# Attention in a decoder step: half a period of lead for the scores, two heads' sums in turn, log weights in the softplus tile

## The reference, cut to what matters

```
z     = einsum('bqhd,bkhd->bhqk', qb, kb) * scale + bias
log_1m = where(mask, log_sigmoid(-z), 0.0)                      # mask: k_pos < q_pos
log_w = log_sigmoid(z) + cumsum(log_1m, reverse=True) - log_1m
w     = where(mask, exp(log_w), 0.0)
out   = einsum('bhqk,bkhd->bqhd', w, vb)
```

## Time and profile before

| | us |
|---|---|
| median of 3 executions | 2448.33 (2446.66 to 2449.82) |
| the profiled execution | 2448.8 |
| its span | 2447.1 |
| PE busy | 2401.9 |
| DVE busy | 1224.1 |
| ACT busy | 999.7 |
| the attention stretch of the loop, in the span | about 573 to 662 |

### The profile page before, as it was taken

How to read it: one execution, slowest core, us unless ns; L and a number is a source line. 1 busy time by engine, 2 the same in 40 slices (tenths; PEclk the granted TensorE clock), 3 DMA queues, 4 the chain that set the end, 5 groups by cost and what they waited for, 6 DMA issues and landing times.

```text
span 2447.1 us, 44037 instructions
## 1 busy us (share of the span) xinstructions
PE 2401.9 (98%) x18930; PEld 2185.9 (89%) x18930; DVE 1224.1 (50%) x1693; ACT 999.7 (41%) x1408; POOL 114.6 (5%) x232
## 2 busy tenths in 40 slices
PE   6999999999999999999999999999999999999998
PEld 4999999965699999999999999887777999999998
DVE  4533335755576332357533346745555657633345
ACT  4522234635466322346422245533223546522243
POOL 0000000121100000000000000011222100000000
PEclk8999999999999999999999999999999999999999
DMA  7555455775546654565755345554455456643254
GB/s 279 180 164 172 127 183 178 254 214 130 191 119 208 199 164 130 179 210 174 240 158 171 117 156 179 193 161 158 159 176 165 134 167 187 186 142 94 86 178 154
DMA packets 122660, 417.12 MB, mean 170 GB/s; under 512 B 23386, under 2 KB 27610, under 8 KB 122210
## 3 DMA queue, kind: packets, MB, share of 16 engines
q1 hardware_dynamic: 89538, 302.08, 39.1%
q10 hardware_dynamic: 17568, 61.87, 7.4%
q0 software_dynamic: 15360, 50.34, 6.3%
HBM read 390.84 MB, written 23.41 MB: 169 GB/s over the span
## 4 chain that ended last, share of the span: by engine, by line
PE 90%; DVE 4%; DMA 2%; ACT 2%; issue 1%; SPq 0%; POOLq 0%; POOL 0%; ACTq 0%; DVEq 0%
PE PS L1986 73%; PE PS L1381 3%; PE PS L1920 3%; PE PS L1950 2%; PE PS L1311 1%; DVE WL L2259 1%; DMA AFIRST<-in_w_ada 1%; PE PS L747 1%; PE PS L1265 1%; PE PS L1296 1%; PE PS L1306 1%; PE PS L1277 1%; PE PS L750 1%; PE PS L1360 1%; ACT WH L2089 1%
## 5 line engine op out<-in xcount | busy, mean ns | idle before, releaser
L2259 DVE TENSOR_TENSOR WL<-RAW,WH 128x1024 fp32r<-128x1024 f32 (+1 forms) x478 | 633.2, 1325 | 702.0 <-ACT WH L2089 701.5
L1986 PE MATMUL PS<-HH,WH 128*128 128x260 f32 x3432 | 800.6, 286 | 3.5 <-DVE QRS L1613 2.2
L1986 PE MATMUL PS<-HH,WL 128*128 128x260 f32 x3432 | 786.7, 283 | 0.0
L1986 PE MATMUL PS<-HL,WH 128*128 128x260 f32 x3368 | 770.4, 283 | 0.0
L2089 ACT ACTIVATE WH<-RAW 128x1024 fp32r<-128x1024 f32 (+1 forms) x478 | 542.5, 1136 | 413.8 <-PE PS L1986 274.2
L1986 PEld LDWEIGHTS PS<-HH,WH 128*128 128x128 f32 x3432 | 569.5, 188 | 38.1 <-issue 30.4
L1986 PEld LDWEIGHTS PS<-HH,WL 128*128 128x128 f32 x3432 | 569.7, 189 | 0.0
L1986 PEld LDWEIGHTS PS<-HL,WH 128*128 128x128 f32 x3368 | 557.9, 188 | 0.6 <-issue 0.2
L1986 PE MATMUL PS<-GH,WH 128*128 128x260 f32 x1408 | 387.3, 285 | 0.0
L1986 PE MATMUL PS<-GL,WH 128*128 128x260 f32 x1408 | 384.6, 283 | 0.0
L1986 PE MATMUL PS<-GH,WL 128*128 128x260 f32 x1408 | 383.9, 283 | 0.0
(11 more groups left out here) (334 smaller groups left out, 2321.8 us busy)
## 6 DMA issues: line engine op xcount, KB each, us to landing
RAW<-in_w_in SPq DMA_DIRECT2D x236, 512.0 KB, 3.6
RAW<-in_w_out SPq DMA_DIRECT2D x120, 704.0 KB, 4.1
AW<-in_w_ada ACTq DMA_DIRECT2D x114, 512.0 KB, 4.5
RAW<-in_w_odd SPq DMA_DIRECT2D x60, 512.0 KB, 3.6
RAW<-in_w_odout SPq DMA_DIRECT2D x30, 512.0 KB, 3.9
RAW<-in_w_even SPq DMA_DIRECT2D x28, 512.0 KB, 4.3
KV<-in_v_pages POOLq DMA_DIRECT2D x32, 256.0 KB, 4.7
SR<-in_ret_past POOLq DMA_DIRECT2D x32, 256.0 KB, 3.8
```

The source lines that it names most:

```text
L1986: last = nc.tensor.matmul(ps[:, x, 0:HT], w[:, k * P:(k + 1) * P], src[k0 + k][:, x, :], start=(begin and t == 0), stop=(end and t == 2))
L2259: nc.vector.tensor_tensor(low_, RAW[:, from_:from_ + w], high_.bitcast(F32), ALU.subtract).then_inc(lo_done, 1)
```

## The change

It does three things in the even layer's attention, and moves no work to another engine.

1. `log_weights` writes its result into `SP`, over the softplus values of the same block, instead of back into `ZS`; `weights` then works in place. So `ZS[h % 4]` is free for the scores of the pair two later as soon as the log weights of the same block have been taken.
2. `scores` run half a period further ahead: blocks 0 and 1 of pair t+2 are computed in the second half of period t, and blocks 2 and 3 of pair t+1 in the first half. `scores(1, 0)` and `scores(1, 1)` come before the loop.
3. The sums of a pair's two heads alternate block by block, each head with its own bank of `PS[1]`. Before, head 2t had its four blocks in the first half, and head 2t+1 in the second. `sum_rank(h, i)` gives the place of a sum in that order. The number of sums, scores, copies, table loads and DMAs stays the same.

Beside it, the output DMA of `UP` (whose place `ZD` takes) gets a semaphore of its own, `pool_out`, and is issued ahead of the `KP` output, and the copy into `ZD` waits for it alone.

```diff
         def biased_to(t, j):
-            return 8 if (t, j) == (1, 0) else 10 * t - 4 if j == 0 else 10 * t - 2 + 2 * j
+            return 4 * t + 4 if t < 1 else 10 * t + 2 * j
+        def sum_rank(h, i):
+            return 8 * (h // 2) + 2 * i + h % 2
+        def bank_free_at(t, j):
+            return biased_to(t, j - 1) if j else 8 if t == 1 else biased_to(t - 1, 3)
...
             def scores(t, j):
-                if t == PAIRS:
+                if t >= PAIRS:
                     return
-                pe.wait_ge(z_dve, biased_to(t, j))
+                pe.wait_ge(z_dve, bank_free_at(t, j))
...
-                n = 4 * h + i
+                n = sum_rank(h, i)
                 pe.wait_ge(lw_done, n - 1) if n >= 2 else pe.wait_ge(vp_evac, 4)
-                last = nc.tensor.matmul(PS[1][:, i % 2, 0:LEN[i]], TRI[:], SP[h % 4][:, OFF[i]:OFF[i] + LEN[i]],
+                last = nc.tensor.matmul(PS[1][:, h % 2, 0:LEN[i]], TRI[:], SP[h % 4][:, OFF[i]:OFF[i] + LEN[i]],
...
             scores_of_one()
+            scores(1, 0)
             ada_step("start", 0)
+            scores(1, 1)
             for t in range(PAIRS):
-                scores(t + 1, 0)
+                scores(t + 1, 2)
                 sums(2 * t, 0)
-                scores(t + 1, 1)
+                scores(t + 1, 3)
+                sums(2 * t + 1, 0)
                 if t:
                     values(t - 1)
                 sums(2 * t, 1)
-                scores(t + 1, 2)
-                sums(2 * t, 2)
+                sums(2 * t + 1, 1)
                 if t == 2:
                     gather(0)
-                scores(t + 1, 3)
-                sums(2 * t, 3)
+                scores(t + 2, 0)
                 if t < 3:
                     values_past(t)
                 ada_step("head", 2 * t)
-                for i in range(4):
-                    sums(2 * t + 1, i)
+                sums(2 * t, 2)
+                sums(2 * t + 1, 2)
+                scores(t + 2, 1)
+                sums(2 * t, 3)
+                sums(2 * t + 1, 3)
                 if t == 3:
                     values_past(3)
                 ada_step("head", 2 * t + 1)
...
             def weights(h):
-                act.wait_ge(lw_done, 4 * h + 4)
-                nc.scalar.activation(SP[h % 4], ZS[h % 4], ACT.Exp).then_inc(w_done, 1)
+                act.wait_ge(lw_done, sum_rank(h, 3) + 1)
+                nc.scalar.activation(SP[h % 4], SP[h % 4], ACT.Exp).then_inc(w_done, 1)
...
-                dve.wait_ge(s_done, 4 * h + i + 1)
-                z = ZS[h % 4][:, OFF[i]:OFF[i] + LEN[i]]
-                nc.vector.tensor_tensor(z, z, PS[1][:, i % 2, 0:LEN[i]], ALU.subtract).then_inc(lw_done, 1)
+                dve.wait_ge(s_done, sum_rank(h, i) + 1)
+                at_ = slice(OFF[i], OFF[i] + LEN[i])
+                nc.vector.tensor_tensor(SP[h % 4][:, at_], ZS[h % 4][:, at_], PS[1][:, h % 2, 0:LEN[i]],
+                                        ALU.subtract).then_inc(lw_done, 1)
...
-                if j == 0:
-                    after(dve, w_done, 2 * t - 2)
-                    if t == 1:
-                        dve.wait_ge(out_done, 96)
+                if (t, j) == (1, 0):
+                    dve.wait_ge(pool_out, 16)
                 for e in range(2):
+                    after(dve, lw_done, sum_rank(2 * t - 4 + e, j) + 1 if t > 1 else 0)
                     dve.wait_ge(z_done, 8 * t + 2 * j + e + 1)
...
             scored_one()
+            scored(1, 0)
+            scored(1, 1)
             nc.vector.tensor_copy(VSR[0:NS, :], PS[3][0:NS, 1, :]).then_inc(vs_ok, 1)
...
-                scored(t + 1, 0)
+                scored(t + 1, 2)
                 log_weights(2 * t, 0)
-                scored(t + 1, 1)
+                scored(t + 1, 3)
+                if t == 0:
+                    softplus(1)
+                log_weights(2 * t + 1, 0)
+                sized(t + 1, 0)
+                sized(t + 1, 1)
+                for e in range(2):
+                    log_weights(2 * t + e, 1)
                 if t:
                     low(t - 1)
...
+                scored(t + 2, 0)
                 ada_evac("head", 2 * t)
-                for i in range(2):
-                    log_weights(2 * t + 1, i)
+                for e in range(2):
+                    log_weights(2 * t + e, 2)
+                scored(t + 2, 1)
+                for e in range(2):
+                    log_weights(2 * t + e, 3)
                 if t < 3:
                     softplus(2 * t + 2)
```

31 lines of the change are left out of this document (11 added, 20 removed).

## The result

| us | before | after |
|---|---|---|
| median of 7 executions | 2448.33 (2446.66 to 2449.82) | 2458.43 (2455.44 to 2463.81) |
| profiled execution, span | 2448.8, 2447.1 | 2457.74, 2456.1 |
| first sum over cached keys (`ZN`) to first output projection | 90.8 | 100.7 |
| the rest of the span | 2356.3 | 2355.4 |

The ratio of the times is 1.0042, with a 95% interval from 1.0032 to 1.0052. The kernel is slower, by more than 0.2% even at the lower end of that interval. The forecast was 2453.9 us, the range ended at 2457.3. The direction was right, and the loss of 10.1 us is nearly twice the 5.6 forecast. The third line of the table says that, in the profiled executions, all of it lies in the stretch that the change touches (I call it the loop).

The account below looks back on a forecast made before the run. PE's list was taken to bound the attention stretch: new waits 10.0 us, less 3.8 of old waits and 0.6 of switches, net +5.6 on the profiled 2448.8, 0.5 lower for the median: 2453.9 us, range 2449.3 to 2457.3.

Parts of the forecast that it names:

- What bounds it, and the log weights in place: Attention stretch: PE's list bounds it, only its waits can be won; writing log weights into `SP` costs nothing.
- The start, +4.65: Start of the loop: PE waits 0.55, 0.5 and 1.2 us around pair 1's score blocks, 2.4 for head 1's softplus.
- The slices, +2.7: Conditioning steps: `w_ada` slices land late, by 1.0 us in the first period, 0.8 then 0.9 in the third.
- Softplus at the turn, +1.35: Turn into the third period: PE waits 1.35 us for a softplus behind both heads' last sums.
- DVE in the third period, +0.9: Third period: PE's next score block waits 0.9 us behind DVE's second softplus, OSM copy and score copies.
- Alternation: Sums of both heads: banks free 0.1 us late four times, +0.4; fewer switches between scores and sums, -0.6.
- What was to go, -3.8: Old PE waits between 572 and 662 us that disappear: 1.5, 1.0, 0.3, and 1.0 of weight loads.
- The step that failed: the clock, +3.4: Loop: the forecast sum counted no loss from half clock, leaving that to a rival.
- Rival B: Start of the loop: the clock falls in the new 2.4 us wait, losing up to 3.4 us, 2457.3; chance 0.09.
- A (the lead holds): From the second period on, later waits (5.35 us) vanish and only the start costs: 2448.6 us; chance 0.18.
- C: Conditioning steps: slices collide with POOL's page loads, two steps wait 1.7 us longer each, 2457.3; chance 0.07.
- D: Start of the loop: early banks are free in time too, so the kernel gets faster, 2446.3 us; chance 0.04.

Follow-up runs that it names:

- the start regrouped: Changed kernel with head 1's softplus ahead of the first log weight, and the v row's copy and bank clearing ahead of pair 1's score copies; 2456.34 us.
- all three regroupings: Changed kernel with head 1's softplus and v row copy early, third-period gather and its copy early, each period's first conditioning step before its second sums; 2451.7 us.
- the steps early: Changed kernel with each period's first conditioning step moved ahead of its second pair of sums; 2455.5 us.
- the alternation alone: Kernel before with log weights in place and a pair's two heads' sums taking turns, score blocks left in their old period; 2457.58 us, ratio 1.0032.
- the lead alone: Kernel before with log weights in place and scores half a period ahead, sums still head by head; 2450.79 us, ratio 1.0007.
- the order without the waits: Changed kernel's instructions with PE and DVE lists reordered so every step's producer is done early; 2441.99 us, ratio 0.9969 to the kernel before.
- the two kernels with added products: Unread products put in PE's waits: ten in the changed kernel, 2455.24 us; six in the one with early softplus, gather and conditioning steps, 2451.76 us.

## Why the prediction was wrong, point by point

- **What bounds it, and the log weights in place.** Right. Everything happened in PE's waits in the loop, and the in-place edit alone measured no difference.
- **The start, +4.65.** Nearly right. Forecast 0.55, 0.5, 1.2 and 2.4; measured 0.52, none, 1.23 and 2.28, together 4.03. The second was covered: the score block and the conditioning step in front ran at half clock and gave DVE its time. With the clock up there it was 0.57 (the start regrouped). The sign that was to prove this step wrong, a first sum of head 0 before 581 us, did appear (580.68), but the whole loop starts 2.8 us earlier in this execution; counted from its first product that sum starts after 12.3 us, and the forecast was 11.1.
- **The slices, +2.7.** Forecast 1.0, then 0.8 and 0.9; measured 0.29 and 0.61, then 0.69 and 0.60, 2.2 together. In the first period the lateness fell on both slices of the step, not on the second alone. Mechanism right, size 0.5 too high.
- **Softplus at the turn, +1.35.** Measured 1.09, with 0.44 in front of it for a bank.
- **DVE in the third period, +0.9.** Measured 0.78.
- **Alternation.** Two waits of 0.2 for log weights instead of 0.4 in four. PE's busy time rose by 3.0 where the clock took 3.4 by estimate, which leaves 0.4 for the switches; forecast 0.6. No run shows this term by itself: all three regroupings together, at full clock and with a few more switches, are busy 86.14 us, 0.2 more than the kernel before.
- **What was to go, -3.8.** This was 0.7 too much. It counted 1.0 us in which weight loads waited for log weights like waits of PE, but PE's own products went on meanwhile. The waits of its products that went are 0.99, 1.48 and 0.34, 2.8 together, and with all smaller gaps at most 3.1 of the loop's idle time.
- **Missed: the copy of the gathered rows, +1.1.** The prediction weighed the OSM copy and the jam of DVE at the start of this period, but not what stands behind them. It listed what each moved DVE instruction lets go for scores and sums, and left out `copy_turned`, which lets go the cached values. Counting every wait of PE against the new DVE list would have shown it: |z| twice, two log weights and `low` are 4.5 us of work (631.71 to 636.17) in front of it. Moving the copy back took the wait away.
- **The step that failed: the clock, +3.4.** The sum took TensorE at full clock throughout, and put the half clock at nothing. The runs showed two stretches of 3.4 us at half clock, by which PE's busy time rose by 3.0, and added products that kept it at 1.00. Rival B had that loss (3.4 us) and came nearest with 2457.3, but by luck: it gave itself a chance of 0.09 and meant one long stretch at the one long wait, and its sign, a clock below 1.00 between 585 and 600 us, did not appear. At 584 to 588 us the clock stayed at 1.00 in the changed kernel; it fell at 574.1, after waits of 1.1 and 0.2 us and within one of 0.5, and at 645.8 behind 0.2, 0.7 and 0.6, with PE's products in between. The reading of the earlier trace rows, that a wait of 2.2 leaves the clock alone, is right of that wait in that execution. It doesn't carry over to several short ones. In other kernels of this study the clock fell behind the long wait after all (at 584.8 with the steps early, at 581.5 in the alternation alone), and in neither of these had it fallen earlier in the loop.
- **The sum.** Waits were forecast at +6.2 and came out at +6.9. That they are so close is partly luck: the new ones came to 10.0 as forecast, but only with the 1.1 that was missed, since the rest was 1.1 under; and 3.1 went in place of 3.8. The busy time adds 3.0, the clock's 3.4 less 0.4: 9.9 us for the loop.

A page's rule bears on the failed step. The Trainium skill (TensorE: Matmul & The Clock Gate, section "A second HAM failure mode: psum-queue depth-cycling") says that a kernel that cycles its outputs through PSUM banks idles for short times between groups of matmuls often enough that the clock goes back and forth. The trace agrees in part: each of the waits at 572 to 574 us is for a bank of PSUM that DVE has yet to empty. The waits ahead of the second fall are mostly for slices. The prediction cited the same page for long gaps only.

Of the other rivals: A (the lead holds) is refuted by the run of the lead alone, which kept its own bank waits, and by the waits in the second half. C is refuted by the landings: the two slices took 3.6 and 4.4 us in the first period and 3.5 and 4.3 in the third, no longer than the 3.6 and 4.6 of the sum. D needed no early bank waits, and there were two new ones, 0.52 and 1.23.

What stays open is which pattern of waits brings the clock down. Six kernels have the same waits of 1.1, 0.2 and 0.52 us at the start. In their profiled executions the clock fell within or just behind the 0.52 in three, behind the 1.23 in one, behind the 2.40 in one, and not at all in the last (all three). Four kernels have the two slice waits of about 0.6 to 0.9 us at the end of the third period; it fell there in two. So a cluster of short waits goes with a fall in some executions and not in others, and a profile of one execution tells only that it can happen. The six loops without a fall are those of the kernel before, of the in-place edit, of all three regroupings, of the order without the waits, and of the two kernels with added products. A run with one long wait of set length, and another with the same idle time in pieces, was not made.

## What to carry to other kernels

Before an order is changed, list for each waiting instruction what it waits for in the new lists, small copies included, and how much now stands in front; here the waits at the places that were laid out came out within 0.3 us each (the slices, two steps, within 0.5 together), but for one of 0.5 that the half clock covered, and the one of 1.1 that was missed was not laid out. If the kernel leaves PE several short waits close together, allow up to 1.7 us for a half-clock stretch behind each such cluster in the upper end of the range, or order the work so that there are none; the order without the waits has a loop 5.2 us shorter and a time 7 us below the kernel before. Running a producer further ahead does nothing for a consumer that was already served; ask for each wait which of the two lists is late.

## What the runs showed of the hardware

- In some profiled executions the granted clock fell to half for about 3.4 us at or behind clusters of waits of 0.2 to 1.2 us, with PE's own work in between; in others the same waits left it at 1.00. One wait of 2.28 us left it at 1.00, one of 2.40 was followed by a fall 0.7 us after its end, and one of 3.02 us by a fall 1.3 us after its end. This row is of the alternation alone:

```profile
582.00:585.40 3.40, 3.40 (x11) 2.47 (x9) 0.69 (x1) 0.00 (x0) 0.00 (x0) 0.57 0.00 0
```

- Ten added products, whose results nothing uses, took the ratio from 1.0042 (1.0032 to 1.0052) to 1.0023 (1.0014 to 1.0032), and the mean granted clock from 0.9940 to 0.9960.
- A half clock hides as well as costs: with the step before it slow, PE's next wait of 0.57 us did not appear. It is missing in the three profiled executions with a fall there, and present in the three that have PE's same order and no fall there.
